# Writing out the layer loop, and taking tile 1's sum of squares one column block later

## The reference

```python
for l in range(DEPTH):                                   # DEPTH = 2
    h = rms_norm(x, norm_mix[l])
    proj = jnp.einsum('bsd,de->bse', h, w_in[l])
    q_a, k_a, v_a, u_b, q_c, k_c, v_c, g_c = jnp.split(proj, IN_SPLITS, axis=-1)
    y_a = sliding_window_sink_attention(q_a, k_a, v_a, q_norm[l], k_norm[l], sinks[l])
    y_b = multiscale_pool(u_b, pool_w[l], pool_scale[l])
    y_c = retention(q_c, k_c, v_c, g_c, pos)
    x = x + jnp.einsum('bse,ed->bsd', jnp.concatenate([y_a, y_b, y_c], axis=-1), w_out[l])
    x = x + moe_ffn(rms_norm(x, norm_ffn[l]), router_w, router_b, w_gate[l], w_up[l], w_down[l])
```

## Time and profile before

| | |
|---|---|
| median of 3 runs | 3096.15 us (3095.84 to 3096.74) |
| the profiled execution: its time, its span | 3080.51 us, 3078.7 us |
| granted TensorE clock, mean | 0.995 |
| TensorE busy | 3024.9 us, 98% |
| VectorE, ScalarE, GpSimd busy | 1392.4, 616.8, 1054.7 us |
| chain that ended last | TensorE 92%, DMA 2%, VectorE 2% |

### The profile page before, as it was taken

One profiled execution on the slowest core, in us unless ns is written; L12 is line 12 of the kernel. 1 busy time (PEld: TensorE's weight loads), 2 busy tenths in 40 slices (PEclk: granted clock), 3 DMA queues, 4 the chain that ended last, 5 costly groups with the idle time before them and its releaser, 6 DMA issues.

```text
span 3078.7 us, 54755 instructions
## 1 busy us (share of the span) xinstructions
PE 3024.9 (98%) x18160; PEld 2161.1 (70%) x18160; DVE 1392.4 (45%) x3996; ACT 616.8 (20%) x1930; POOL 1054.7 (34%) x1250
## 2 busy tenths in 40 slices
PE   8999999999899999999989999999999999999998
PEld 3455555555799999888745555555557999998887
DVE  5576677667322222211155766776674222221111
ACT  1322322323111111110123223223231111111101
POOL 1232132233255555432212321331332555554322
PEclk9999999999999999999999999999999999999999
DMA  8756656653789999999875566566537899999996
GB/s 302 260 189 246 236 188 243 230 185 128 269 288 310 310 332 346 345 348 350 287 259 191 199 227 241 198 229 241 188 137 252 299 306 304 345 340 346 351 351 221
DMA packets 248473, 817.19 MB, mean 265 GB/s; under 512 B 68304, under 2 KB 120528, under 8 KB 189264
## 3 DMA queue, kind: packets, MB, share of 16 engines
q1 hardware_dynamic: 200480, 733.80, 64.6%
q0 software_dynamic: 46112, 77.70, 10.9%
q10 hardware_dynamic: 1584, 2.00, 0.2%
HBM read 718.95 MB, written 95.56 MB: 265 GB/s over the span
## 4 chain that ended last, share of the span: by engine, by line
PE 92%; DMA 2%; DVE 2%; issue 1%; SPq 1%; ACT 0%; POOL 0%; DVEq 0%; ACTq 0%; POOLq 0%
PE bank L2125 31%; PE bank L1827 19%; PE bank L1892 14%; PE bank L2165 9%; PE bank L2155 6%; PE bank L1798 4%; PE bank L1726 3%; PE bank L1979 1%; PE bank L2020 1%; PE bank L2054 1%; DMA arena<-in_x 1%; PE bank L1903 1%; DMA arena<-out 0%; PE bank L1988 0%; DVE arena L1243 0%
## 5 line engine op out<-in xcount | busy, mean ns | idle before, releaser
L2125 PEld LDWEIGHTS bank<-arena,wts 128*128 128x128 f32 x8192 | 983.8, 191 | 18.4 <-issue 18.4
L2125 PE MATMUL bank<-arena,wts 128*128 128x128 f32 (+7 forms) x8192 | 988.0, 283 | 4.2 <-issue 4.2
L1827 PE MATMUL bank<-wts 128*128 128x512 f32 x1056 | 469.5, 596 | 0.0
L1892 PE MATMUL bank<-wts,arena 128*128 128x512 f32 x1024 | 453.9, 596 | 1.7 <-ACT arena L1073 1.6
L1701 DVE TENSOR_TENSOR arena<-arena,bank 128x128 f32<-128x128 f32 (+6 forms) x64 | 19.2, 300 | 903.7 <-ACT arena L1135 903.7
L1827 PEld LDWEIGHTS bank<-wts 128*128 128x128 f32 x1056 | 194.9, 190 | 219.7 <-issue 218.1
L835 POOL DMA_INDIRECT arena<-hrows,arena x288 | 290.2, 1008 | 167.6 <-issue 150.3
L1892 PEld LDWEIGHTS bank<-wts,arena 128*128 128x128 f32 x1024 | 189.4, 190 | 216.6 <-issue 214.2
L731 POOL TENSOR_TENSOR arena<-arena 128x256 f32<-128x256 f32 x32 | 25.4, 795 | 859.2 <-DVEq L1437 859.2
L861 POOL DMA_INDIRECT out<-arena x176 | 275.1, 1563 | 54.7 <-issue 52.1
L2165 PE MATMUL bank<-arena,wts 128*128 128x135 f32 (+6 forms) x2176 | 280.1, 289 | 0.0
(11 more groups left out here) (273 smaller groups left out, 3123.5 us busy)
## 6 DMA issues: line engine op xcount, KB each, us to landing
wts<-in_w_gate SPq DMA_DIRECT2D x128, 1024.0 KB, 8.2
wts<-in_w_up SPq DMA_DIRECT2D x128, 1024.0 KB, 11.2
wts<-in_w_down SPq DMA_DIRECT2D x128, 1024.0 KB, 17.3
wts<-wt SPq DMA_DIRECT2D x96, 1024.0 KB, 5.9
wts<-in_w_in SPq DMA_DIRECT2D x88, 1024.0 KB, 7.3
hrows<-arena SPq DMA_DIRECT2D x36, 512.0 KB, 5.7
out<-arena SPq DMA_DIRECT2D x36, 512.0 KB, 3.2
wt<-arena SPq DMA_DIRECT2D x16, 1024.0 KB, 4.5
```

The source lines that it names most:

```text
L1827: i = mm(bIP[j in (1, 3, 6)][:, :], own[:, d], ring[k % SLOTS][:, d], start=(d == 0 and j in (0, 1, 3)), stop=(d == 3), skip_group_check=True)
L1892: i = mm(bIP[k][:, :], dT[o][:, d - 4] if d in (4, 5) else mixT[:, d], wout[:, d, 512 * k:512 * k + 512], start=(n == 0), stop=(n == DC - 1))
L2125: return mm(gu_at(f, k, w), lhs, xT[:, d, 0:w], start=start, stop=(d == DC - 1), skip_group_check=True)
```

## The change

The outer loop is written out by Python on all five engines, `for l in range(DEPTH)`; choices between the layers are made while the program is written, and waits have fixed values. The inner loop over the rounds of experts stays. Apart from this, in step 0 the sum of squares of tile 1 trades places with one column block of tile 0: on TensorE it comes behind block 2 instead of block 1, on ScalarE it comes behind the taking out of block 1 instead of block 0.

```diff
-            with e.Fori(0, DEPTH) as l:
+            for l in range(DEPTH):
...
-                    with e.If(l == 0):
+                    if l == 0:
...
@@ ScalarE, step 0
                     if s == 0:
                         sumsq_first()
                         whole_columns(0, 0)
+                        whole_columns(0, 1)
                         sumsq_front(1)
-                        for n in range(1, 4):
-                            whole_columns(0, n)
+                        whole_columns(0, 2)
+                        whole_columns(0, 3)
                         sumsq_front(2)
@@ TensorE, step 0
                         whole(0, 0)
                         whole(0, 1)
+                        whole(0, 2)
                         sumsq(1)
-                        whole(0, 2)
                         whole(0, 3)
```

More of the change, by code:

```diff
@@ L464, in _ @@
             e.reg_mov(halves, 0)
-            with e.Fori(0, DEPTH) as l:
+            for l in range(DEPTH):
                 h0 = e.snap(halves)
                 def load_x(dst, full, t):
-                    with e.If(l == 0):
+                    if l == 0:
                         e.dma_start(dst, x[rows(t), :]).then_inc(full, 16)
-                    with e.Else():
+                    else:
                         e.dma_start(dst, out[rows(t), :]).then_inc(full, 16)
@@ L494, in _ @@
                 wait_alone(e, down_done, h0 * 2 + 1)
-                with e.If(l > 0):
+                if l > 0:
                     e.dma_start(gmix8, small[bass.ds(l, 1), :, 828:836].rearrange("o p n -> p (o n)")).then_inc(gmix8_full, 16)
```

## The result

| | before | after |
|---|---|---|
| median | 3095.48 us (3092.89 to 3096.74, 20 runs) | 3100.59 us (3094.32 to 3105.44, 20 runs) |
| profiled execution: its time, its span | 3080.51, 3078.7 us | 3099.09, 3097.2 us |
| granted clock, mean | 0.995 | 0.996 |

The ratio after to before is 1.0017, with a 95% interval of 1.0010 to 1.0024: 5.1 us slower. The forecast was 1.4 us faster. The time lies inside the range that was given, but the sign was wrong, and the interval leaves it no room.

A forecast was written before the change was run, and what follows sets the result against it. It took layer 0 to hang on when VectorE gets tile 1's sum, not on TensorE's products. Layer 0 +5.7, boundary and layer 1 -6.3, ends -0.8 gave -1.4 us: 3094.7 us, range 3087.5 to 3103.5.

The forecast's parts named there:

- The sum of tile 1 in layer 0 at 35.7 (34 to 37): Layer 0, step 0: tile 1's sum of squares, behind block 2, comes at 35.7 instead of 29.37, 6.3 us later.
- The fourth sum of layer 0 later by 5.7, chain as before: Layer 0: the 6.3 us delay carries over VectorE's queue to the fourth sum, less 0.6 for register instructions: 5.7 lost.
- No stop of TensorE, SyncE's gap gone, both leading to little by themselves: Layer boundary: SyncE's 4.5 us gap goes with the jump; TensorE's gain of 4.2 to 5.1 leads nowhere by itself.
- The scattered add 5.2 us earlier: Layer boundary: layer 0's last add ends at 1544.5 instead of 1549.75, bounds 0 and 8; row norm and pieces follow.
- no wait would stand ahead of block 2: Layer 1: block 2 starts at once at 1556.6 with the clock up; tile 1's sum follows 3.5 us earlier.
- Layer 1's fourth sum 6.3 earlier: Layer 1: fourth sum 6.9 us earlier, 0.6 taken back for a clock fall: gains 6.3, bounds -8 and +2.
- The ends of the mixing parts -0.8, and no fall of the clock behind the waits added: Ends of both mixing parts: register waits go for -0.8 us, bounds 0 and -2; layer 0's new waits priced at nothing.
- The terms of layer 0 and of the boundary: Layer 0 loses 5.7 us; the boundary together with layer 1 gains 6.3 us.
- they replace the wait removed; they are not added: Layer 0: TensorE's many new waits, about 4 us at the fourth sum among them, add nothing to the time.
- register waits: Ends of the two mixing parts, where last adds and router fold are waited for: -0.8 us, bounds 0 and -2.
- Rival 1: Boundary: SyncE's gap isn't the jump, or the scattered add is slow by itself; +3.9, 3100 us; chance 0.19.
- rival 2: VectorE's delayed queue start carries in both layers, clock low until 33.5 in layer 0; +8.4, 3104.5 us; chance 0.14.

The follow-up runs named there:

- the order alone: Kernel before with only step 0's new order on ScalarE and TensorE, loop over layers kept: 3086.33 us, ratio 1.0030, 8.1 us slower.
- the kernel whose clearing was moved: Changed kernel with SyncE's clearing of rows in layer 0 moved behind step 1's first loads: 3099.01 us, ratio 1.0010 to the kernel before.
- the loop alone: Kernel before with the layer loop written out on all engines, old order: 3074.5 us, ratio 0.9992; again 3096.75 us, ratio 1.0003.
- the early sum alone: Against before: loop written out, tile 1's pieces asked for sooner and its sum one block earlier in layer 0, old order in layer 1: 3095.72 us, ratio 0.9997.
- the fourth comparison: Four kernels timed against shared runs of the kernel before, which took 3117.84 us; the changed kernel took 3119.45 us there, ratio 1.0007.
- the first and third comparison: Two groups of four runs, each timed against shared runs of the kernel before, which took 3078.25 us and 3096.13 us.
- the second and fourth: Two groups of four runs, each timed against shared runs of the kernel before, which took 3096.46 us and 3117.84 us.

## Why the forecast was wrong

By its own steps, with the three profiles of the changed kernel and three of the old order with its loop kept.

*The sum of tile 1 in layer 0 at 35.7 (34 to 37).* 34.90, 32.85 and 32.77. The direction was right, and the cause (block 2's weights, then 16 products) in the first of the three. Too late by 1 to 3 us: SyncE, without the loop's registers, issued block 2's weights at 5.41 to 5.70 instead of 6.66, and they landed 1.3 to 2.4 us earlier where I gave 0.3. In the second and third profile they landed before TensorE had ended block 1, so that it neither waited nor fell in clock there; what made their sums later than the weights alone would have is that the first six records of block 0 took 0.8 to 1.2 us each, where the first profile has 0.6 to 0.7.

*The fourth sum of layer 0 later by 5.7, chain as before.* The chain is the one forecast, link for link. The size is +3.3 on the means: the first sum came 4.9 us later, not 6.3, and from it to the fourth the changed kernel took 68.2 us in all three profiles where the kernel before's loop has 69.0 to 70.5, so that 1.6 us were taken up on the way and not 0.6. With the loop kept, the order alone was 7.9 us later than the one profile beside it and 6.7 later than the mean; with the loop written out in both it costs 3.1 on the means (3.7 without the kernel whose clearing was moved).

*No stop of TensorE, SyncE's gap gone, both leading to little by themselves.* Right, and each gap belongs to its own engine's loop. This is where the Trainium skill (Runtime: NRT & Kernel Launch, Instruction fetch mechanics) was weighed: by that rule the gap goes with the jump, and the runs agree, at 4.7 us for SyncE and 6.1 for TensorE with the loop, and 0.4 and 0 without. That an engine fetches in its gap they don't show.

*The scattered add 5.2 us earlier.* 2.7 in the profile after, so the row norm still held block 2 up, by 3.06 us. That no wait would stand ahead of block 2 was wrong. The sum still came at the forecast distance from expert 31 (28.85 against 28.9), because TensorE began block 0 3.1 us sooner than I had it: 1.0 is the first of its two stops, of which I had taken off only the second, and 2.1 the turnings, which in the earlier trace rows had run at a lowered clock behind the stop (0.84 in the mean of that stretch); I had carried that over. Two errors that cancel are not a confirmation.

*Layer 1's fourth sum 6.3 earlier.* 6.4 on the means. Right, though most of it (3.8) comes with the loop alone, in whose kernel I had not looked for it.

*The ends of the mixing parts -0.8, and no fall of the clock behind the waits added.* This is the step that failed. What lies behind the fourth sums got longer by 1.9 and 3.4 us, +5.3 where I had -0.8: 6.1 us. The terms of layer 0 and of the boundary had erred by 2.4 us the other way; without the 6.1 the stretches would add up to -3.9 and not to +2.2. Three things are in it. The first is the half clock behind the new or longer waits at the fourth sums: 2.4 us a profile in layer 0 against 2.2 before, and 1.7 in layer 1 against 0 (means of the table above). I had written of the waits in layer 0 that "they replace the wait removed; they are not added", and priced a fall of the clock only for the one ahead of the scores in layer 1, with 0.6. The second is the writing out, which makes the last folds slower by 1.1 us in layer 0 and 1.3 to 1.7 in layer 1, the falls of the clock taken off. Part of it can be placed: with all five engines written out TensorE reaches two of the folds 0.3 and 1.0 us later than before (612.2 and 650.0 us behind the fourth sum of layer 1 against 611.9 and 649.0) behind new waits for VectorE's line 1521. With TensorE's program alone written out they aren't there. Why VectorE is later there has not been found. The third is the clock in the last folds, four falls in the three profiles of the changed kernel and three in those of before's loop, and a matter of chance as far as these profiles tell. That "register waits" would go at these places was an assumption; no row showed them.

The rivals: none came true as it stood. Rival 1's time, +3.9, came nearest to the +5.1, but by luck: it left layer 1's fourth sum where it was, and that sum came 6.4 us earlier. Its place (a slow scattered add) was half right, rival 2's carry-over in both layers wrong in layer 1, and the naive reading of the waits (-21) as far off as its low chance said.

So in the changed kernel layer 0 loses about 5 us and layer 1 wins about 3, and the times (+5.1, +6.4, +1.6) lie around or above the sum of +2.2. That the mean of the timed ones, +4.4, is 2 us more is within what the profiles scatter, and not explained further. What is shown is that the order is the loss (+8.1 with the loop kept), that the loop by itself is not told from nothing (-3.75 and +0.6), and that the same sum taken one block earlier in layer 0 instead of later, its pieces asked for sooner, turns the sign: -6.1 and -3.9 us. That kernel beats both. With the old order in layer 1 the early sum alone was not told from before (-0.7 us).

## What to carry to other kernels

A wait that is exchanged for one later in the chain is not exchanged at par: price what TensorE's clock does behind it, and look at every wait that the faster engine will newly meet. Before moving a small product behind a large one, ask who starts from the small one's result; here VectorE's queue of 70 us did, and the way to gain was to feed it sooner, not to keep TensorE busy longer. Cut the span at fixed events and compare stretches over several profiles, since one profile's places scatter by as much as such a change is worth.

## What the runs showed of the hardware

The same program took 3078, 3096 and 3118 us in different comparisons, and the step lies in the experts' parts: 731.2 and 741.7 us in the run of before in the first, 739 to 742 and 749 to 752 in the second and third, 749 to 751 and 759 to 762 in the fourth. There TensorE waits more for nothing that the profile shows ahead of its products (before 4.2 us in all, 3 times); in the changed kernel of the fourth comparison:

```profile
PE bank L2126 <- issue: 17.7, 38, 1.4
```

These waits make up 13.5 of the 38 us between the two. What sets this level was not found; it moves all kernels alike. It isn't the chip alone: the first and third comparison ran on one chip (3078 and 3096 us), the second and fourth on another (3096 and 3118 us). Both profiles of the kernel before are of the lowest level and all three of the changed kernel of the two higher ones, so a part of the differences in the last folds may belong to the level: there the loop alone takes 635.4 and 635.6 us in the first comparison and 635.9 and 636.1 in the third.

The end of the outer loop, with its jump back over a layer's body, cost SyncE 4.1 to 4.7 us and TensorE two stops, of 0.8 to 2.0 and of 4.1 to 4.6 us, each in that engine alone. The scattered add took 9.8 to 14.0 us beside the loads of weights, and 5.0 with the queues empty. SyncE's reload, which waits for it (line 509), is issued 15.0 to 16.0 us behind expert 31 in the four profiles that keep SyncE's loop, and 11.8 to 13.6 us in the thirteen with all loops written out, where the weights start some 4 us earlier: 3.1 us on the means.
